# Inverse roots of all norms as exp(-log(x)/2) on ScalarE, in place of ScalarE's root and VectorE's reciprocal

## The reference, cut to what matters

```python
def rms_norm(x, w):
    return x * (mean(x * x, -1) + eps) ** -0.5 * w
```

## Time and profile before

| | |
|---|---|
| median of 3 runs | 2411.84 us (2411.57 to 2415.27) |
| profiled execution | 2407.98 us, of which the span 2406.1 us |
| busy: TensorE, VectorE, ScalarE, GpSimd | 94%, 64%, 45%, 34% |
| mean granted clock of TensorE | 0.971 |

### The profile page before, as it was taken

The page is one execution under the profiler, slowest core; times in us unless marked ns, Lnnn a source line. Parts: engine busy times, 40 slices in busy tenths (PEclk is TensorE's granted clock), DMA queues, the critical chain, the costliest instruction groups (busy, mean ns, idle before and its releaser), DMA issues.

```text
span 2406.1 us, 41252 instructions
## 1 busy us (share of the span) xinstructions
PE 2254.8 (94%) x16556; PEld 2089.2 (87%) x16556; DVE 1537.6 (64%) x2647; ACT 1077.2 (45%) x1983; POOL 813.6 (34%) x738
## 2 busy tenths in 40 slices
PE   6999999899989999999799899997999999888998
PEld 5878679889987787699799899987899999887997
DVE  5866567598777765686898764377644644437443
ACT  4554322455446453323555544414544544445443
POOL 2441102136435531121255243244442343132441
PEclk9999899999999998999999999998999999999999
DMA  6773248546765742386367655643456556533554
GB/s 223 199 196 103 94 169 300 185 147 214 251 227 152 215 134 84 134 293 241 132 219 247 209 169 183 185 138 116 163 186 179 172 184 182 164 123 132 184 180 127
DMA packets 121949, 429.27 MB, mean 178 GB/s; under 512 B 14959, under 2 KB 16927, under 8 KB 121632
## 3 DMA queue, kind: packets, MB, share of 16 engines
q1 hardware_dynamic: 94208, 333.80, 41.8%
q0 software_dynamic: 27408, 91.77, 13.1%
q10 hardware_dynamic: 144, 1.07, 0.1%
HBM read 425.48 MB, written 1.10 MB: 177 GB/s over the span
## 4 chain that ended last, share of the span: by engine, by line
PE 84%; DVE 10%; ACT 4%; issue 2%; POOL 0%; DMA 0%; SPq 0%; DVEq 0%; ACTq 0%
PE bank L375 21%; PE bank L377 21%; PE bank L376 20%; PE bank L740 5%; PE bank L365 3%; PE bank L463 2%; DVE u L1544 2%; DVE ring_lo L1556 2%; PE bank L440 1%; DVE std L1580 1%; PE bank L455 1%; PE bank L557 1%; PE bank L394 1%; ACT ring_hi L885 1%; PE bank L599 1%
## 5 line engine op out<-in xcount | busy, mean ns | idle before, releaser
L375 PE MATMUL bank<-x_hi,ring_hi 128*128 128x256 f32 (+2 forms) x3040 | 885.2, 291 | 47.5 <-DVE x_lo L2194 13.9
L1556 DVE TENSOR_TENSOR ring_lo<-ring,ring_hi 128x1024 fp32r<-128x1024 f32 (+1 forms) x436 | 585.3, 1344 | 486.1 <-ACT ring_hi L885 485.9
L376 PE MATMUL bank<-x_lo,ring_hi 128*128 128x256 f32 (+2 forms) x3040 | 873.8, 287 | 0.0
L377 PE MATMUL bank<-x_hi,ring_lo 128*128 128x256 f32 (+2 forms) x3040 | 873.4, 287 | 0.0
L885 ACT ACTIVATE ring_hi<-ring 128x1024 fp32r<-128x1024 f32 (+1 forms) x550 | 567.2, 1034 | 327.4 <-PE bank L377 245.5
L2311 POOL TENSOR_TENSOR ring_lo<-ring,ring_hi 128x1024 fp32r<-128x1024 f32 (+1 forms) x156 | 398.4, 2554 | 773.8 <-ACT ring_hi L885 497.6
L375 PEld LDWEIGHTS bank<-x_hi,ring_hi 128*128 128x128 f32 x3040 | 584.2, 192 | 67.2 <-issue 28.8
L377 PEld LDWEIGHTS bank<-x_hi,ring_lo 128*128 128x128 f32 x3040 | 584.8, 192 | 0.0
L376 PEld LDWEIGHTS bank<-x_lo,ring_hi 128*128 128x128 f32 x3040 | 583.2, 192 | 0.5
L377 PE MATMUL bank<-hid_hi,ring_lo 128*128 128x256 f32 (+1 forms) x1056 | 299.8, 284 | 0.0
L375 PE MATMUL bank<-hid_hi,ring_hi 128*128 128x256 f32 (+1 forms) x1056 | 298.6, 283 | 0.0
(11 more groups left out here) (316 smaller groups left out, 2932.7 us busy)
## 6 DMA issues: line engine op xcount, KB each, us to landing
ring<-in_w_gu SPq DMA_DIRECT2D x192, 512.0 KB, 3.5
ada_ring<-in_ada POOLq DMA_DIRECT2D x144, 512.0 KB, 5.0
ring<-in_w_in SPq DMA_DIRECT2D x136, 512.0 KB, 4.4
ring<-in_ffn_up SPq DMA_DIRECT2D x104, 512.0 KB, 3.5
ring<-in_w_down SPq DMA_DIRECT2D x64, 512.0 KB, 3.5
ring<-in_w_branch SPq DMA_DIRECT2D x32, 512.0 KB, 4.3
ring<-in_ffn_down SPq DMA_DIRECT2D x32, 512.0 KB, 5.0
ring<-in_w_down SPq DMA_DIRECT2D x32, 384.0 KB, 3.3
```

Source lines behind the costliest of these rows:

```text
L375: pe.matmul(b[:, cs], ring_hi[:, i_hi, c0], x1, start=first and k == 0, stop=False)
L376: pe.matmul(b[:, cs], ring_hi[:, i_hi, c0], x2, start=False, stop=False)
L377: m = pe.matmul(b[:, cs], ring_lo[:, i, c0], x1, start=False, stop=last and k == nk - 1)
L1556: dve.tensor_tensor(ring_lo[:, i, 0:cols], ring[:, i, 0:cols], ring_hi[:, n % HIGH, 0:cols].bitcast(f32), ALU.subtract).then_inc(split(n)[ ...
```

## The change

Each root becomes two instructions on ScalarE: Ln of sum/dim + eps out of the bank, signalled as "log", then, behind a wait for it, Exp of -1/2 times that in place, signalled as "inverse". The reciprocals and their waits leave VectorE, which waits for "inverse" alone. TensorE's claims that waited for "std" wait for "log". `use_tables(ACT.Sqrt)` becomes `use_tables(ACT.Ln)` in most places; others are taken out: Exp after the top norm, Exp after the first decay logs, Sqrt ahead of the A roots and Exp behind the latents', and the Sqrt and Exp around the B roots. The second `use_tables(ACT.Exp)` behind the decay logs of the second pair and the one ahead of the block attention become Ln.

```diff
-                ps = claim(NB, act_, "std", *norm_name)
+                ps = claim(NB, act_, "log", *norm_name)
...
             def low_root(b, i, name, dim):
                 act.wait_ge(*at(pe_, "norm", *name))
-                act.activation(low_stat[i], bank[b][:, 0:T], ACT.Sqrt, scale=1.0 / dim, bias=eps_ap).then_inc(*sig(act_, "std", *name))
+                act.activation(low_stat[i], bank[b][:, 0:T], ACT.Ln, scale=1.0 / dim, bias=eps_ap).then_inc(*sig(act_, "log", *name))
+                act.wait_ge(*at(act_, "log", *name))
+                act.activation(low_stat[i], low_stat[i], ACT.Exp, scale=-0.5).then_inc(*sig(act_, "inverse", *name))
 
             def root(b, i, name, dim, cs, *reader):
+
                 act.wait_ge(*at(pe_, "norm", *name))
                 before(("std", i), dve_, *reader)
-                act.activation(std[:, i, cs], bank[b][:, cs], ACT.Sqrt, scale=1.0 / dim, bias=eps_ap).then_inc(*sig(act_, "std", *name))
+                act.activation(std[:, i, cs], bank[b][:, cs], ACT.Ln, scale=1.0 / dim, bias=eps_ap).then_inc(*sig(act_, "log", *name))
+                act.wait_ge(*at(act_, "log", *name))
+                act.activation(std[:, i, cs], std[:, i, cs], ACT.Exp, scale=-0.5).then_inc(*sig(act_, "inverse", *name))
...
                     high_parts(2 * k + 2, 2 * k + 3)
-                use_tables(ACT.Exp)
                 act.wait_ge(*at(dve_, "lam", l, 1))
...
                 decay_logs(l, 0)
-                use_tables(ACT.Exp)
                 vt_a_of(l, 0)
...
                 halves(("bq", l, 1))
-                use_tables(ACT.Sqrt)
                 latent_squares(l)
...
                 low_root(7, 1, ("kvlat", l), 128)
-                use_tables(ACT.Exp)
...
                 decay_logs(l, 1)
-                use_tables(ACT.Exp)
+                use_tables(ACT.Ln)
...
                     if hd == 1:
-                        use_tables(ACT.Sqrt)
                         root_b(l, 0, 0)
...
                         root_b(l, 1, 1)
-                        use_tables(ACT.Exp)
...
                     if j == KD - 1:
-                        use_tables(ACT.Sqrt)
+                        use_tables(ACT.Ln)
...
                 for j in range(4):
                     act.wait_ge(*at(pe_, "var", j))
-                    act.activation(std[:, j, 0:N2], bank[2 + j][:, 0:N2], ACT.Sqrt, bias=eps_ap).then_inc(*sig(act_, "ln_std", j))
+                    act.activation(std[:, j, 0:N2], bank[2 + j][:, 0:N2], ACT.Ln, bias=eps_ap).then_inc(*sig(act_, "ln_log", j))
+                    act.wait_ge(*at(act_, "ln_log", j))
+                    act.activation(std[:, j, 0:N2], std[:, j, 0:N2], ACT.Exp, scale=-0.5).then_inc(*sig(act_, "ln_inverse", j))
...
-            def recip(i, name, cs=ALL):
-                dve.wait_ge(*at(act_, "std", *name))
-                dve.reciprocal(std[:, i, cs], std[:, i, cs]).then_inc(*sig(dve_, "recip", *name))
-                dve.wait_ge(*at(dve_, "recip", *name))
+            def inverse_root(i, name, cs=ALL):
+                dve.wait_ge(*at(act_, "inverse", *name))
                 return std[:, i, cs]
...
             def latent_norms(l):
-                for i, name in enumerate((("qlat", l), ("kvlat", l))):
-                    dve.wait_ge(*at(act_, "std", *name))
-                    dve.reciprocal(low_stat[i], low_stat[i]).then_inc(*sig(dve_, "recip", *name))
-                dve.wait_ge(*at(dve_, "recip", "kvlat", l))
+                dve.wait_ge(*at(act_, "inverse", "kvlat", l))
...
-                    dve.wait_ge(*at(act_, "ln_std", j))
-                    dve.reciprocal(std[:, j, 0:N2], std[:, j, 0:N2]).then_inc(*sig(dve_, "ln_rs", j))
-                    dve.wait_ge(*at(dve_, "ln_rs", j))
+                    dve.wait_ge(*at(act_, "ln_inverse", j))
```

More of the change, by code:

```diff
@@ L427, in norm_gathered @@
             def norm_gathered(name, last, cs=ALL):
-                ps = claim(NB, act_, "std", *name)
+                ps = claim(NB, act_, "log", *name)
                 pe.wait_ge(*at(dve_, "gathered", *name))
@@ L561, in norm_a @@
             def norm_a(l, hd):
-                norm(6 + hd % 2, ("oa", l, hd), [hd], [("sqa", ("A", l, hd))], (act_, "std", "oa", l, hd))
+                norm(6 + hd % 2, ("oa", l, hd), [hd], [("sqa", ("A", l, hd))], (act_, "log", "oa", l, hd))
             def norm_b(l, p, hh):
-                norm(6 + hh, ("ob", l, p, hh), [4 + 2 * p + hh], [("sqb", ("B", l, p), hh)], (act_, "std", "ob", l, p, hh))
+                norm(6 + hh, ("ob", l, p, hh), [4 + 2 * p + hh], [("sqb", ("B", l, p), hh)], (act_, "log", "ob", l, p, hh))
             def latent_q(l, hd):
@@ L681, in mixers @@
                 project(("bk", l, 1), ALL, (act_, "k", B[1]))
-                norm(6, ("qlat", l), [6, 7], [("sqlat", l, 0), ("sqlat", l, 1)], (act_, "std", "qlat", l))
-                norm(7, ("kvlat", l), [5], [("sqlat", l, 2)], (act_, "std", "kvlat", l))
+                norm(6, ("qlat", l), [6, 7], [("sqlat", l, 0), ("sqlat", l, 1)], (act_, "log", "qlat", l))
+                norm(7, ("kvlat", l), [5], [("sqlat", l, 2)], (act_, "log", "kvlat", l))
                 chunk_states(B[0])
@@ L802, in conv_mixers @@
                 for j in range(4):
-                    b = claim(2 + j, act_, "ln_std", j)
+                    b = claim(2 + j, act_, "ln_log", j)
                     pe.wait_ge(*at(dve_, "ya", j))
@@ L1658, in latents @@
                 dve.tensor_scalar(nsk, par(l, "sinks", 0, 8), -1.0, None, ALU.mult).then_inc(*sig(dve_, "nsk", l))
-                rs = recip(2, ("top", l))
+                rs = inverse_root(2, ("top", l))
                 scaled(("lat", l, 0), rs)
@@ L2004, in ffn @@
                     gather(("out", l), ("sqo", l), j - 1, cs)
-                rs = recip(0, ("out", l), cs)
+                rs = inverse_root(0, ("out", l), cs)
                 for k in range(KD):
@@ L2008, in ffn @@
                 low_halves("up", l, 0, 0)
-                rs = recip(1, ("ffn", l), cs)
+                rs = inverse_root(1, ("ffn", l), cs)
                 def divided(*ks):
@@ L2070, in ffn @@
                     gather(("down", l), ("sqd", l), j - 1, fs)
-                rs = recip(0, ("down", l), fs)
+                rs = inverse_root(0, ("down", l), fs)
                 if l < DEPTH - 1:
@@ L2108, in sublayer_input @@
             def sublayer_input(s, cut):
-                rs = recip(0, ("in2", s), TEXT)
+                rs = inverse_root(0, ("in2", s), TEXT)
                 base = (s // 3) * 72 + (s % 3) * 24
@@ L2295, in vector_program @@
             swiglu(3)
-            rs = recip(0, ("in2", 6), TEXT)
+            rs = inverse_root(0, ("in2", 6), TEXT)
             for k in range(KD):
```

4 lines of the change are left out of this document (2 added, 2 removed).

## The result

The changed kernel takes 2460.59 us (median of 4 runs, 2455.77 to 2462.1), the kernel before 2412.57 in the same runs (2411.57 to 2415.27). The ratio is 1.0194, with a 95% interval of 1.0176 to 1.0211: 48 us slower. The profiled execution took 2461.91 us, of which the span 2460.1; the mean granted clock is 0.961 where it was 0.971.

A forecast was written before the change was run, and what follows sets the result against it. The prediction took TensorE, 94% busy, to bound the kernel, other engines counting only where it waits. Its terms summed to +39.7 us on the profiled 2407.98, or 2451 from the median; own range 2438 to 2466, with rival 3 2436 to 2468.

The forecast's parts named there:

- (a): Nine single roots on the chain: load and Exp replace the reciprocal, 0 to -0.1 us each, -0.9.
- (b): Six roots with a Silu or Gelu load behind (four swiglus, two ffn): load no longer hidden, +6.6 us.
- (c): Six roots near the heads' end: chunk_states waits for the last Ln, +10.1 and +9.1, together +19.3 us.
- (d): Four B-head roots around the third mixer's copies: latent_v waits for the last Ln, both layers +10.7 us.
- (e): Group norm: loads between its four roots and ahead of the Silus end the stage later, +5.8 us.
- (f): Table loads saved after both top norms, one moved behind layer 1's decay logs: -3.8 us.
- (g): New idle of TensorE lowers its clock at restarts: +2 us in all, bounds 0 and 8.
- 1 (one set): One table set serves Ln and Exp, no load between: about 21 us faster, 2391; chance 0.05.
- 2 (covered): At the run of six and B heads, other TensorE slabs cover ScalarE's lateness: 2420 us; chance 0.07.
- 3 (the stalls cost more than themselves): Clock at its bound (+6) and late queues missing later slabs (+4 to +9): 2466 us; chance 0.13.
- 4 (drain): Each load on the path also stops the engine for the load's length: +72 us, 2523; chance 0.01.

The follow-up runs named there:

- borders_only: The changed kernel with only the fifteen single roots as Ln and Exp; roots standing in rows keep ScalarE's root and VectorE's reciprocal. 2414.2 us, ratio 1.0006.
- six_only: The kernel before with Ln and Exp only for the run of six roots (four A heads, two latents) in both layers. 2437.9 us, ratio 1.0121.
- loads_only: The kernel before, roots and reciprocals unchanged, with Exp and Sqrt tables exchanged between the six roots of the row. 2440.3 us, ratio 1.0114.
- filled: The changed kernel with 26 matmuls of constants (7 and 19) on TensorE in the stalls up to chunk_states, both layers. 2460.5 us, ratio 1.0205.
- filled_less: The changed kernel with 15 matmuls of constants (4 and 11) on TensorE in the stalls up to chunk_states. 2451.7 us, ratio 1.0165.
- logs_first: The changed kernel with all Ln ahead of all Exps in each row of roots, 58 loads in place of 96. 2413.5 us, ratio 1.0002.
- one_set: The changed kernel, root order unchanged, with the table set holding both Ln and Exp loaded by name, 31 loads. 2390.6 us, ratio 0.9913.

## Why the prediction was right, and the term that was too small

The forecast was 2451 (2436 to 2468) and slower at 0.92; measured 2460.6. The mechanism was as forecast: 96 loads, and stalls of TensorE of the lengths that the sum gives. By its own steps:

- **(a) single roots, -0.9.** Right, near nothing: the four stretches of the first stack between such roots changed by +0.2, -0.5, +0.2 and -0.3.
- **(b) roots with a Silu or Gelu load behind, +6.6.** Slightly large: 3.6 for the four swiglus in borders_only, 1.0 and 0.8 for the two ffn in the changed kernel, 5.4 in all. The path is not quite the one I had drawn. VectorE's three low parts do not wait for GpSimd's half to be through; counted from the root they start 0.4 later than before, run beside it and take 1.78 for 1.27 (the row below the list, before). TensorE waits there too, 1.5 us for a low half that comes late, and waits 0.7 less a little later. That in the changed kernel three swiglus are 2.4 us longer and one 0.9 is the clock (below).
- **(c) the run of six, +19.3.** Right as a stall: 10.16 and 9.2 where 10.1 and 9.1 stood. six_only shows the place and loads_only the cause.
- **(d) B heads, +10.7.** Right as a stall: 5.4 and 5.5 in the traces.
- **(e) group norm, +5.8.** Right: 15.7 for 9.9 in the trace.
- **(f) saved, -3.8.** Slightly small: in the traces the run of six began 1.85 and 3.0 earlier, the second counted from the root behind `down`.
- **(g) the clock, +2 with bounds 0 and 8.** This is the term that failed in size: it came to some 14, beyond its upper bound of 8. TensorE's busy time that the lower clock accounts for rose from 52.9 to 69.3 us. Matching the instructions of the two traces, the stretches behind chunk_states lost 2.3 and 4.5 by it; the swiglus lost 4.5 (8.1 longer, less the 3.6 of (b)), which is three dips more at 1.5; in the pair mixer the brackets grew by 2.7. The first two, 6.8, stand behind the new stalls. That the other 7.2 are an effect of the change is not shown: filled and filled_less have the same code in these stages, with two dips more than before in the swiglus and none more, and logs_first, without the stalls, has the long pair mixer too. I had looked only at the places where TensorE restarts behind a new stall, took each for 4 us at half clock, and halved the result for dips already nearby. What I had not seen is that waits of before, unchanged, can turn into a dip too; what decides it stays open.

VectorE's timeline of the changed kernel at the first swiglu, for (b):

```profile
1419.48 1.78 DVE L1545 SCALAR_TENSOR_TENSOR x_lo<-u,mod,x_hi 128x256 fp32r<-128x256 f32 x3 [2.50 <-ACT x_hi L1415]
```

The last point of (g) in one example: the start of the first swiglu, windows of 12 us, in the changed kernel and then in filled, whose code for this stage is the same.

```profile
1425.60:1437.60 12.00, 8.98 (x61) 8.63 (x61) 10.27 (x19) 4.84 (x9) 5.51 (x6) 0.86 0.34 109
```

```profile
1422.70:1434.70 12.00, 8.98 (x73) 8.63 (x73) 10.26 (x19) 5.55 (x9) 5.52 (x6) 1.00 0.40 125
```

TensorE's waits up to its restart stand at the same distance from the root in both, within 0.02 us, and the last, 2.3 us ahead of the first divided slabs, is in the kernel before as well (2.29); in one the restart is granted 0.86 in the mean and the stage takes 193.9, in the other 1.00 and 192.4. A dip there is worth 1.5 us. The changed kernel had it in all four swiglus, the kernel before in one.

With (g) at 14 in place of 2, (b) at 5.4 and (f) at -4.9 the sum is 49.4; the medians differ by 48.0, the stages of the two profiles by 50.2. That the number held is in part luck: (g) alone went 6 us beyond its bound, and the time, 9 above the forecast, stayed in the range because (b) and (f) came out 2.3 better than forecast and the other terms used little of their width. The 3.9 us that I added from the profile to the median are found too: the second profile of before has them, 2.8 in the convolution, 0.6 in the pairs and 0.5 ahead of the first root.

Of the rivals, **1 (one set)** did not happen by itself, 96 loads tell that, but is true of the chip: named, the set serves both, and one_set took 2390.6 where the rival's sum said 2391. The Trainium skill (ScalarE: Activation LUTs, Rules for kernel authors) says that one set holds both functions; the traces agree once the load is explicit (31 loads), and not for the loads that the program gets when only functions are named (96). **2 (covered)** is out by the 5.9 us wait at L540. **3 (the stalls cost more than themselves)** is half right: the time came out 9 above the forecast, by the clock, but no new wait for a slab stands behind the stalls in the trace. **4 (drain)** is out: 0.01 to 0.02 us stand beside the loads, but for eight behind which ScalarE waits for a norm, and the single roots stayed as long, which leaves no room for a stop beside the load's own 1.28.

## What to carry to other kernels

Count table exchanges in the built program, not functions in the source: Ln, Exp, Ln, Exp cost 1.28 us at each step until a set with both was named, and then the same instructions made the kernel 0.9% faster. If no set serves both, put all of one function first: what counted in these rows is how many loads stand ahead of the instruction that releases a bank, since TensorE worked on beside the load behind it. Replacing a 1.8 us reciprocal by a load and an Exp gains nothing. Replacing it by the Exp alone shortened the four stretches of the first stack between single roots by 1.4 to 1.9 us (one_set); a swiglu, where a Silu load stands behind the root, was shorter by 0.3 only (192.7 for 193.1, both at full clock).

## What the hardware did that I had not expected

- **Dips of TensorE's clock are worth 1.5 us each in a swiglu and come and go with the same waits.** Swiglus of one code are 192.35 and 193.87 us, without and with a dip. Over the twelve profiles the lower clock accounts for 52 to 69 us of TensorE's busy time; the kernel before, in its two profiles, has the least, and the changed kernel the most.
- **A shorter way to a wait can cost the clock behind it.** Coming to latent_v at full clock, TensorE waited 2.4 us and then ran at 0.50; coming there late, it waited 1.03 and stayed at 1.00.
- **VectorE's taps and GpSimd's work on other tiles seem to hold each other up.** A group of 29 taps takes 11.56 us or 12.79 to 16.36, by how GpSimd's six passes over the same mixer fall. GpSimd's timeline in the second profile of before:

```profile
1603.29 0.65 POOL L2522 TENSOR_TENSOR br<-br 128x256 f32<-128x256 f32 x1 [2.90 <-ACT br L1475]
...
1617.10 8.95 POOL L2522 TENSOR_TENSOR br<-br 128x256 f32<-128x256 f32 x1 [8.38 <-ACT br L1475]
...
1631.82 0.74 POOL L2522 TENSOR_TENSOR br<-br 128x256 f32<-128x256 f32 x1 [0.83 <-ACT br L1475]
```

The same instruction takes 0.65 or 0.74 us while VectorE's groups take 14.79 and 16.36, and 8.95 in the group that takes 11.56, where it ends half a microsecond behind the last tap. Which of the two takes longer differs between two executions of one kernel, and is worth 3 us in the stage. That they hold each other up is read from these lengths; I did not test it, nor what the two engines share.
